# A block pair in fp32 on one core: modulation sums handed out after every weight split, or after every pair of splits

## The reference

```python
def _modulation(cvec, w, b):
    m = jax.nn.silu(cvec) @ w + b
    ...
def first_block(...):
    ...
    f = rms_norm(h, g_ffn_pre[l])
    f = jnp.square(jax.nn.relu(f @ w_ff1[l])) @ w_ff2[l]
    h = h + rms_norm(f, g_ffn_post[l])
def _attention_layer(...):
    shift, scale, gate = _modulation(c, mod_w, mod_b)
    shift_c, scale_c, gate_c = _modulation(c_ctx, mod_w, mod_b)
    h = _rmsnorm(x, pre_g) * (1 + scale) + shift
    hc = _rmsnorm(ctx, pre_g) * (1 + scale_c) + shift_c
    ...
```

## Time and profile before

| quantity | value |
|---|---|
| median of 3 runs | 1944.54 us (1942.66 to 1945.73) |
| the profiled execution | 1945.73 us |
| its span, first to last instruction | 1944.0 us |
| PE busy | 1847.5 us (95%) |
| DVE busy | 1423.5 us (73%) |
| ACT busy | 906.9 us (47%) |
| mean granted TensorE clock | 0.984 of full |

### The profile page before, as it was taken

One profiled execution on the slowest core, in us unless ns is written; L12 is line 12 of the kernel. 1 busy time (PEld: TensorE's weight loads), 2 busy tenths in 40 slices (PEclk: granted clock), 3 DMA queues, 4 the chain that ended last, 5 costly groups with the idle time before them and its releaser, 6 DMA issues.

```text
span 1944.0 us, 30240 instructions
## 1 busy us (share of the span) xinstructions
PE 1847.5 (95%) x11648; PEld 1667.1 (86%) x11648; DVE 1423.5 (73%) x1597; ACT 906.9 (47%) x1203; POOL 118.8 (6%) x217
## 2 busy tenths in 40 slices
PE   6999999799999999999999979998999997999997
PEld 6999978699889988988998767776888787999976
DVE  5799987668878887888788967543677666686754
ACT  5444556444444444444444365422556545444452
POOL 0000000000110000000000000000111000000000
PEclk9999999999999999999999989998999998999999
DMA  8855436668887787768878664544444584677652
GB/s 288 269 194 187 157 133 249 228 199 282 318 309 263 244 267 256 251 225 267 263 243 290 224 220 150 182 141 152 154 151 149 205 277 143 221 234 262 210 189 88
DMA packets 185304, 424.57 MB, mean 218 GB/s; under 512 B 8192, under 2 KB 8576, under 8 KB 183680
## 3 DMA queue, kind: packets, MB, share of 16 engines
q1 hardware_dynamic: 157568, 322.69, 49.1%
q0 software_dynamic: 27648, 100.68, 15.7%
HBM read 419.14 MB, written 4.19 MB: 218 GB/s over the span
## 4 chain that ended last, share of the span: by engine, by line
PE 82%; DVE 10%; ACT 3%; DMA 2%; issue 2%; SPq 0%; DVEq 0%; POOL 0%; POOLq 0%; ACTq 0%
PE acc L1508 13%; PE acc L1510 13%; PE acc L1509 13%; PE acc L1521 12%; PE acc L1523 12%; PE acc L1522 12%; DVE w_lo L916 3%; DVE mod_sum L1049 2%; PE aux L1549 2%; PE aux L1743 1%; DMA mod_raw<-in_ev_mod_w 1%; DVE scratch L1174 1%; PE aux L1756 1%; PE aux L1734 1%; PE acc L1756 1%
## 5 line engine op out<-in xcount | busy, mean ns | idle before, releaser
L478 ACT ACTIVATE w_hi<-raw 128x1024 fp32r<-128x1024 f32 x552 | 577.2, 1057 | 719.9 <-PE acc L1510 366.9
L916 DVE TENSOR_TENSOR w_lo<-raw,w_hi 128x1024 fp32r<-128x1024 f32 x552 | 667.6, 1224 | 320.5 <-ACT w_hi L478 319.4
L1508 PE MATMUL acc<-a_hi,w_hi 128*128 128x256 f32 x2304 | 657.1, 285 | 4.2 <-DVE a_lo L1013 2.5
L1510 PE MATMUL acc<-a_hi,w_lo 128*128 128x256 f32 x2304 | 652.3, 283 | 0.0
L1509 PE MATMUL acc<-a_lo,w_hi 128*128 128x256 f32 x2304 | 652.3, 283 | 0.0
L1508 PEld LDWEIGHTS acc<-a_hi,w_hi 128*128 128x128 f32 x2304 | 442.7, 192 | 5.5 <-issue 3.8
L1509 PEld LDWEIGHTS acc<-a_lo,w_hi 128*128 128x128 f32 x2304 | 442.7, 192 | 0.7 <-issue 0.5
L1510 PEld LDWEIGHTS acc<-a_hi,w_lo 128*128 128x128 f32 x2304 | 442.5, 192 | 0.0
L1521 PE MATMUL acc<-w_hi,b_hi 128*128 128x512 f32 x800 | 314.3, 393 | 6.5 <-DVE w_lo L916 6.5
L954 DVE SCALAR_TENSOR_TENSOR mod_sum<-mod_raw,silu_c,mod_sum 128x1024 f32<-128x1024 f32 x240 | 301.8, 1279 | 20.9 <-DMA mod_raw<-in_ev_mod_w 15.4
L1522 PE MATMUL acc<-w_lo,b_hi 128*128 128x512 f32 x800 | 311.9, 390 | 0.0
(11 more groups left out here) (192 smaller groups left out, 1398.4 us busy)
## 6 DMA issues: line engine op xcount, KB each, us to landing
raw<-in_w_ff SPq DMA_DIRECT2D x128, 1024.0 KB, 6.4
mod_raw<-in_ev_mod_w POOLq DMA_DIRECT2D x96, 512.0 KB, 4.5
mod_raw<-in_od_mod_w POOLq DMA_DIRECT2D x96, 512.0 KB, 5.1
raw<-in_w_in SPq DMA_DIRECT2D x40, 1024.0 KB, 5.1
raw<-in_ev_w_in SPq DMA_DIRECT2D x40, 1024.0 KB, 5.1
raw<-in_od_w_in SPq DMA_DIRECT2D x32, 1024.0 KB, 5.6
raw<-in_w_out SPq DMA_DIRECT2D x16, 1024.0 KB, 5.3
raw<-in_ev_w_out SPq DMA_DIRECT2D x16, 1024.0 KB, 7.0
```

The costliest lines, as they stand in the source:

```text
L478: nc.scalar.activation(w_hi[:, s % SLOTS], raw[:, s // 2, KPS * (s % 2):KPS * (s % 2) + KPS, :], ACT.Copy).then_inc(hi_ready, 1)
L916: nc.vector.tensor_tensor(w_lo[:, s % SLOTS], raw[:, s // 2, KPS * (s % 2):KPS * (s % 2) + KPS, :], w_hi[:, s % SLOTS].bitcast(F32), ALU.s ...
L1508: nc.tensor.matmul(o, wh, hi[:, k, :], start=first and t == 0 and f % 2 == 0, stop=False, skip_group_check=True)
L1510: last = nc.tensor.matmul(o, wl, hi[:, k, :], start=False, stop=t == KPS - 1, skip_group_check=True)
```

## The change

The FF stage calls `run_ahead` in place of `each_ahead`: a function after each pair of splits, m = 0 to 3, and counts written out for each block n. `each_ahead` and `spread` are gone. What is handed out is the same in kind and in total, but at other places:

- `ev_gate`: 20 halves ahead of the FF stage in place of 22, and 12 in blocks 0 and 1, as 2, 1, 2, 1 at m = 0 to 3. The turn is at n = 2, m = 0 (same place as p = 17).
- `od_shift`: 0, 2, 2, 1 in block 2; 2, 1, 1, 1 in blocks 3 to 5; 2, 1, 2, 1 in blocks 6 and 7. The turn is at n = 8, m = 0.
- `ev_shift`: 0, 1, 1, 1 in blocks 8 to 18. Its turns are at n = 18, m = 3 and n = 19, m = 0.
- `ev_scale`: 0, 1, 1, 1 in blocks 19 to 29. Its turns are at n = 30, m = 0 and m = 1.
- `od_scale`: six halves in the FF stage in place of two: one at n = 30, m = 3 and 2, 1, 2 in block 31. So evq has 2 in place of 3, evkv 4 and 4 in place of 5 and 6.

Both outputs of `mod_out` stay at n = 17 and n = 25.

```diff
@@ -923,12 +923,6 @@
-            def each_ahead(b, between, last=8):
-
-                for i in range(last):
-                    split_lo(b + (i >= 4), ((4 + i) % STEPS,))
-                    between(i)
-
             def most_ahead(b, between=None):
                 for m in range(3):
@@ -1158,13 +1152,13 @@
             for i in range(3):
                 for f in range(40 + 4 * i, 44 + 4 * i):
-                    if f % 2:
-                        halves("ev_gate", 14 + 2 * i + f % 4 // 2, 1)
+                    if f % 4 == 1:
+                        halves("ev_gate", 14 + i, 1)
             for f in range(52, 58):
-                if f in (52, 54):
-                    halves("ev_gate", 20 + (f - 52) // 2, 1)
+                if f < 55:
+                    halves("ev_gate", 17 + f - 52, 1)
             def add_to_residual():
@@ -1193,45 +1187,45 @@
-            def spread(unit, p, start, num, den, first=0, last=2 * KT):
-
-                done = lambda q: min(max(first + (q - start) * num // den, first), last)
-                halves(unit, done(p), done(p + 1) - done(p))
-
             def ff_mods(n):
-                def go(i):
-                    p = 8 * n + i
-                    if p == 17:
-                        mod_turn("ev_gate", 0, 1, 0, ff_temp)
-                    elif p == 70:
-                        mod_turn("od_shift", 0, 0, 0, ff_temp)
-                    elif p in (157, 158):
-                        mod_turn("ev_shift", p - 157, p - 157, 1, ff_temp)
-                    elif p in (245, 246):
-                        mod_turn("ev_scale", p - 245, p - 245, 2, raw_temp)
-                    elif p < 17:
-                        spread("ev_gate", p, 0, 5, 8, 22)
-                    elif p < 70:
-                        spread("od_shift", p, 18, 5, 8)
-                    elif p < 157:
-                        spread("ev_shift", p, 71, 3, 8)
-                    elif p < 245:
-                        spread("ev_scale", p, 159, 3, 8)
-                    elif 249 <= p < 253:
-                        spread("od_scale", p, 249, 1, 2, 0, 2)
-                    if p == 136:
-                        mod_out(0, [(OD_SHIFT, col("od_mod_b", 0, KT)), (EV_GATE, col("ev_mod_b", 32, KT))])
-                        nc.vector.tensor_tensor(mod_cols[:, EV_GATE, :], mod_cols[:, EV_GATE, :],
-                                                col("ev_post_g", 0, KT), ALU.mult)
-                    if p == 200:
-                        mod_out(1, [(EV_SHIFT, col("ev_mod_b", 0, KT)), (EV_SHIFT_C, col("ev_mod_b", 0, KT))])
+                def go(m):
+                    if n < 2:
+                        halves("ev_gate", 20 + 6 * n + (0, 2, 3, 5)[m], (2, 1, 2, 1)[m])
+                    elif n < 8:
+                        if n == 2 and m == 0:
+                            mod_turn("ev_gate", 0, 1, 0, ff_temp)
+                        else:
+                            each("od_shift", (0, 5, 10, 15, 20, 26)[n - 2], (0, 2, 2, 1) if n == 2 else (2, 1, 1, 1) if n < 6 else (2, 1, 2, 1))(m)
+                    elif n < 19:
+                        if n == 8 and m == 0:
+                            mod_turn("od_shift", 0, 0, 0, ff_temp)
+                        elif m and 3 * (n - 8) + m <= 2 * KT:
+                            halves("ev_shift", 3 * (n - 8) + m - 1, 1)
+                        elif n == 18 and m == 3:
+                            mod_turn("ev_shift", 0, 0, 1, ff_temp)
+                        if n == 17 and m == 0:
+                            mod_out(0, [(OD_SHIFT, col("od_mod_b", 0, KT)), (EV_GATE, col("ev_mod_b", 32, KT))])
+                            nc.vector.tensor_tensor(mod_cols[:, EV_GATE, :], mod_cols[:, EV_GATE, :],
+                                                    col("ev_post_g", 0, KT), ALU.mult)
+                    elif n < 30:
+                        if n == 19 and m == 0:
+                            mod_turn("ev_shift", 1, 1, 1, ff_temp)
+                        elif m and 3 * (n - 19) + m <= 2 * KT:
+                            halves("ev_scale", 3 * (n - 19) + m - 1, 1)
+                        if n == 25 and m == 0:
+                            mod_out(1, [(EV_SHIFT, col("ev_mod_b", 0, KT)), (EV_SHIFT_C, col("ev_mod_b", 0, KT))])
+                    elif n == 30 and m < 2:
+                        mod_turn("ev_scale", m, m, 2, raw_temp)
+                    elif n >= 30:
+                        halves("od_scale", (0, 0, 0, 0, 1, 3, 4)[4 * (n - 30) + m],
+                               (0, 0, 0, 1, 2, 1, 2)[4 * (n - 30) + m])
             def ff_hidden(g):
                 for bi in range(4):
-                    each_ahead(BLOCK["ff"] + 8 * g + bi, ff_mods(8 * g + bi))
+                    run_ahead(BLOCK["ff"] + 8 * g + bi, ff_mods(8 * g + bi))
@@ -1251,7 +1245,7 @@
             def ff_outer(g):
                 for bi in range(4):
-                    each_ahead(BLOCK["ff"] + 8 * g + 4 + bi, ff_mods(8 * g + 4 + bi))
+                    run_ahead(BLOCK["ff"] + 8 * g + 4 + bi, ff_mods(8 * g + 4 + bi))
             def ff_gained(n):
@@ -1266,7 +1260,7 @@
             for n in range(NBLK):
-                each_ahead(BLOCK["ff"] + 28 + n, ff_mods(28 + n), 8 if n < NBLK - 1 else 6)
+                (run_ahead if n < NBLK - 1 else most_ahead)(BLOCK["ff"] + 28 + n, ff_mods(28 + n))
@@ -1314,7 +1308,7 @@
             for n in range(4):
-                run_ahead(BLOCK["evq"] + n, ctx_rms if n == 0 else each("od_scale", 2, (1, 1, 1, 0)) if n == 3 else None)
+                run_ahead(BLOCK["evq"] + n, ctx_rms if n == 0 else each("od_scale", 6, (1, 0, 1, 0)) if n == 3 else None)
@@ -1323,7 +1317,7 @@
             for m in range(2):
-                run_ahead(BLOCK["evkv"] + m, each("od_scale", 5 + 5 * m, (1, 1, 1, 2) if m == 0 else (1, 2, 1, 2)))
+                run_ahead(BLOCK["evkv"] + m, each("od_scale", 8 + 4 * m, (1, 1, 1, 1)))
```

## The result

The changed kernel takes 1960.34 us in the median of 5 runs (1957.01 to 1963.79), the kernel before 1945.73 us (5 runs, 1942.66 to 1947.76). The ratio is 1.0079, with a 95% interval of 1.0064 to 1.0093: slower by 0.8%. The profiled execution took 1962.57 us, its span is 1960.9 us, mean clock 0.979.

What follows compares the result with a forecast made beforehand. PE was taken to set the pace, with DVE's order showing only through PE's waits or the serial chain. The terms 15.9 - 1.0 + 1.0 - 1.2 = +14.7 us on 1945.73 us gave 1960 us, range 1948 to 1971 us.

Steps and rivals of the forecast that it cites:

- The path: Whole FF stage: PE sets the pace; DVE's order shows only in PE's waits or the serial chain at norm or attention.
- The reload as the deciding price: Modulation loads: two halves sharing a buffer start no closer than 7.7 us, or 6.1 us where the half was late.
- Parts 1 and 2: FF blocks 0 to 8, ev_gate and od_shift with their turns: new waits of PE, +15.9 us together.
- A half behind its pair, two in a row: Halves directly behind a finished pair of splits: the reload takes its full 5.8 us landing, so bursts make DVE late.
- Part 3: Turns of ev_shift, the first at n = 18, m = 3: waits of 2.0 us replace 3.1 us, -1.0 us.
- Part 4: Blocks 30 and 31: ev_scale turn waits go (-3.5 us), the last od_scale add comes 4.5 us late: +1.0 us.
- Part 5: evq and evkv: one half instead of two in front of the last rope, where PE waits 5.93 us: -1.2 us.
- The clock: Within (c): a wait of PE lasts so long that the granted clock falls; 0.50 was read behind the 5.93 us wait.
- (a): Rival: loads land fast, 4.2 us for all, as DVE asks at other moments: -3.4 us, 1942 us; chance 0.11.
- (b): Rival: as (a), and the last od_scale half lands before PE ends block 31: -4.7 us, 1941 us; chance 0.07.
- (c): Rival: binding loads take 6.2 to 7.5 us, or the clock falls behind a long wait of PE: 1969 us; chance 0.16.
- (d): Rival: hidden blocks make up the backlog; first bursts and blocks 6, 7 show half as large: +5, 1951 us; chance 0.11.

Runs made afterwards that it cites:

- experiment 1: The changed kernel with each modulation load cut to its first 128 of 1024 columns (64 KB instead of 512 KB): 1934.82 us, ratio 0.9955.
- experiment 2: The kernel before with the same small 64 KB modulation loads, as a control for lighter DMA traffic: 1941.27 us, ratio 0.9986.
- experiment 5: The changed kernel with the same counts in blocks 0 to 7, handed out one half at a time after single splits: 1964.33 us, ratio 1.011.
- experiment 9: The kernel before with blocks 0 to 8 in the change's form (pairs of splits, two halves at m = 0) at the old rate: 1949.32 us, ratio 1.0016.
- experiment 4: The changed kernel with only two od_scale halves in blocks 30 and 31, evq and evkv as before: 1964.47 us, ratio 1.0101.

## Why the prediction was right, and where it was not

- **The path.** PE sets the pace and shows DVE's order only by its waits: right. All that was gained or lost in the FF stage is such a wait or the clock behind one.
- **The reload as the deciding price.** Right, and shown by experiments 1 and 2: 64 KB loads take the waits away. The median landing used, 5.8 us, measured 5.7. The rule of the Trainium skill ("DMA: Bandwidth & Descriptors", "Anatomy of one DMA — SWDGE (gpsimd) path") held no better after than before: an estimate of 3.2 us, where the fastest load from 400 to 600 us took 3.9.
- **Parts 1 and 2: forecast 15.9 us of waits. Measured: 12.6 us of waits, and 18.6 us of delay with the slower matmuls.** The delay is read from PE's first matmul of block 4 and of block 8, first before, then after:

```profile
489.38 0.40 PE L1521 MATMUL acc<-w_hi,b_hi 128*128 128x512 f32 x1
...
576.45 0.28 PE L1508 MATMUL acc<-a_hi,w_hi 128*128 128x256 f32 x1
```

```profile
498.65 0.40 PE L1515 MATMUL acc<-w_hi,b_hi 128*128 128x512 f32 x1
...
592.33 0.28 PE L1502 MATMUL acc<-a_hi,w_hi 128*128 128x256 f32 x1
```

  Counted from the stage's start, block 4 is 9.0 us late (forecast 6.5) and block 8 15.6 us (forecast 10.75); the waits in block 8 add 3.0 (forecast 3.6 + 1.5). The places were right. As waits, step 4 of block 2 cost 3.85 us where 1.9 was forecast, and the 1.5 us forecast behind the turn did not show; step 4 of block 3 cost 1.80 (3.1 forecast), blocks 6 and 7 3.65 and 1.82 (4.25 and 3.6), the turn in block 8 1.20 (1.5). The term that was too small is the reload of the sixth half. I took a landing of 5.8 us for it; in blocks 1, 6 and 7 it was 7.1, 7.6 and 6.8 us (issues at 446.46, 564.78 and 592.77). Block 6 took DVE 27.6 us from its first half (552.06) to that of block 7 (579.65) where I had 26.0. It still cost PE less than forecast, since DVE entered it with some slack: block 5 had ended without a wait, where I had counted from a DVE at its limit.
- **"A half behind its pair, two in a row" as the harm** was my reading of where the cost sits; the ledger itself priced the count as well. Experiments 5 and 9 correct it: pairs at five in a block cost 0.6 us of waits, six in a block cost 12.6 us in pairs and 14.0 one at a time.
- **Part 3:** forecast -1.0, measured 3.1 to 1.8 us, -1.3. Right.
- **Part 4:** the turn waits went, as said (-3.5). The last add came 3.1 us late, not 4.5. The first load behind the turns landed in 4.0 us where I had taken 5.8 (issue at 1115.11), so the first two halves and with them the fourth came some 2.3 us earlier than forecast; the last load then took 4.9 us where I had taken 4.2. -0.4 in place of +1.0.
- **Part 5:** -1.2, measured -1.2.
- **The clock.** I had put it among the rivals, and it came: two waits of over 3.5 us were followed by PE at 0.51 and 0.50 of full clock, and PE's busy time in the stage grew by 6.1 us. The forecast left it out. But these 6 us look like no cost beside the waits. Behind both falls DVE stands only for `mod_raw` and ACT, not for PE, until it releases PE again (487.03 and 605.83). So a PE at full clock would, by this reading, have come there some 2.5 and 3 us sooner and waited for longer: the slow matmuls took the place of waits, and that is why the waits came out smaller than the delay. Experiment 9 shows such a swap behind the first turn of `ev_scale`. Before (first row) and experiment 9 (second), PE busy and granted clock:

```profile
1109.00:1113.00 4.00, 2.31 (x10) 1.59 (x9) 2.78 (x3) 4.00 (x8) 0.00 (x0) 1.00 1.00 380
1109.00:1113.00 4.00, 3.90 (x11) 2.58 (x10) 2.79 (x3) 3.99 (x7) 0.00 (x0) 0.58 0.98 367
```

  Both have a wait of 1.77 us just before (PE goes on at 1107.54 and 1107.90). Before, the second wait of 1.69 us follows, and PE goes on at 1112.26; in experiment 9 the clock falls, there is no second wait, and PE goes on at 1112.61, the same 4.7 us later.
- **The total** of +14.7 us was forecast; it is +16.9 of the profiled spans and +14.6 of the medians. The early blocks were 2.7 us too cheap in the forecast and the tail 1.4 us too dear. The sum was closer than its terms, and that it hits the medians to 0.1 us is luck.
- **The rivals.** (a) and (b), fast loads, are what experiment 1 made by hand. Of (c) both parts came in some measure, the longer landings of late halves and the fall of the clock, but not its price. (d), half of the bursts' price, did not come. That the clock falls behind a wait is shown by the windows; a kernel with these waits and no fall of the clock was not run.

## What to carry to other kernels

Work that waits for its own double-buffered load has a rate limit of its own: two per reload time (add, issue, landing under the traffic of that stretch), however much busy time its engine has left. Compare that with the part of a block in which such work can stand before raising the count in it; in the two orders tried here, the order inside the block mattered little beside it. Where a long piece on the engine that feeds TensorE makes it wait, cut it so that one part fits between two deliveries: together with the shorter wait at the rope that went with 0.44% here.

## What the hardware showed that was not expected

The granted clock fell behind some short waits and not behind others. In the changed kernel a wait of 1.80 us left it at 1.00, those of 3.85 and 3.65 us did not; in experiment 5 it read 0.50 from 489 to 491 us behind a wait of 2.35 us. The wait of 2.85 us in evq (at 1182.58 in the kernel before, at 1200.82 in experiment 5) is the same in both; some 2.3 us behind its end the one read full clock and the other 0.62 over 3 us, the mean of a part at the lower level (half clock) and a part at full:

```profile
1185.00:1188.00 3.00, 3.00 (x15) 2.49 (x14) 2.07 (x2) 1.06 (x1) 0.00 (x0) 1.00 0.95 325
```

```profile
1203.00:1206.00 3.00, 3.00 (x10) 2.33 (x9) 1.08 (x1) 0.56 (x1) 0.00 (x0) 0.62 0.92 304
```

The next wait in evq is 1.97 us in experiment 4 (it ends at 1227.22) and 1.98 in the kernel before (1209.25); the clock behind it read 0.52 from 1229 to 1231 us in the one and 1.00 from 1211 to 1213 in the other. So the length of a wait alone does not tell whether the clock falls; what else decides was not tested. Executions of one kernel differ in their mean clock too: of the ten of experiment 1 the fastest, 1932.95 us, has 0.985 and the slowest, 1943.96 us, has 0.978. And a load of one eighth of the bytes, beside others as small, landed in 3.6 us in the median where the full one took 5.7 us: most of the reload time is not the load's own bytes.
